# The first RMS norm by halves of the tokens, and the first slabs evicted ahead of the decays

## The chip, the core and the metric

The program runs on one core of a Trainium2 chip. The core has five engines with queues of their own, which meet by semaphores alone: TensorE (PE, with its weight loads as PEld), VectorE (DVE), ScalarE (ACT), GpSimd (POOL) and SyncE (SP). SyncE and ScalarE issue the transfers between HBM and SBUF here. The metric is the device time of one execution in microseconds, the median of several runs.

## The reference

Two transformer blocks over 1024 tokens of width 1024 in float32. The change lies at the start of the first. What is computed there:

```python
h = rms_norm(x, mix_norm_g[l])
p = jnp.einsum("btd,de->bte", h, w_in[l])
(gm_u, gm_v, cv_a, cv_g, dn_q, dn_k, dn_v, dn_g,
 dn_beta, dn_alpha) = jnp.split(p, offsets, axis=-1)
y_a = spatial_gating(gelu(gm_u), gelu(gm_v), ...)
...
beta = jax.nn.sigmoid(beta_logit)
log_alpha = -jnp.exp(a_log) * jax.nn.softplus(alpha_logit + dt_bias)
```

with `rms_norm(x, g) = x * rsqrt(mean(x * x) + 1e-6) * g` over the 1024 features of a token. A convolution branch, a chunked gated delta rule, the output projection and a gated feed-forward follow, then a second block (sliding-window attention beside a state-space layer, between two feed-forwards). None of that is touched.

## The kernel before

**Layout.** Features lie on the 128 partitions and tokens on the free axis: x is 8 tiles k (KD = 8) of 128 features by 1024 tokens, behind 16 columns for meta tokens. The tokens are worked on in two halves of 512, CH1, numbered c = 0, 1.

**Products.** A float32 product is made of three matmuls on operands split in two: high parts by a cast (h_hi, w_hi) and the rests (h_lo, w_lo). Weights come in slabs of 128 output features by 1024 inputs, in pairs (i, j) with j = 0, 1, each j with one buffer for w_raw, w_hi and w_lo. SyncE loads w_raw when GpSimd has split what was there (L486). ScalarE makes w_hi when TensorE is done with the j buffer's slab (w_high, L511 to L517; for pair i it waits for acc_full[j] to count every chunk before). GpSimd makes w_lo in four pieces (L547). TensorE then runs 24 matmuls of 512 columns for each half of the tokens (pe_slab, L651 to L653), having waited for w_lo and for the result bank to be evicted (acc_free).

**The order of the work** is the order in which each engine's instructions are written; no scheduler moves them. The start is:

1. SyncE loads constants, parameters and the first two weight slabs; ScalarE issues the loads of x, two k in each.
2. ScalarE squares tile k over all 1024 tokens into one of two sqx buffers (act_squares, L1060), TensorE sums over the partitions with a matmul against a matrix of 1/1024 (L595), for each half into a PSUM bank.
3. ScalarE casts the first two slabs (L517), takes Sqrt of both halves (L605), and then casts h_hi, eight tiles for each half (L609).
4. VectorE takes, for each half, the reciprocal (L615) and x times gain times reciprocal into one of four tmp buffers (the "gain" below, L625), and makes h_lo of tiles 2 and 5 (L629). GpSimd makes the h_lo of the other six (L583), behind the splits of the first two slabs. A gain that reuses a tmp buffer waits for the h_lo of four tiles before.
5. VectorE casts the 8 columns of weights of beta and alpha into ba_hi and makes ba_lo (L1596, L1597).
6. TensorE, for each half c: the logits of beta and alpha (L1113 to L1115, 24 matmuls), then slabs (0,0) and (0,1) of gm for that half (pe_first_pair, L833). Then eight small transposes of the logits (L1123), slabs (1,0) and (1,1) of gm, slab (0,0) of cv, and the decays' sums, for which it waits.
7. ScalarE copies the logits (L1363, L1365), and runs the chain of decays (Sigmoid, Exp, Ln, Exp, L1368 to L1373, with a table load before each, in turn with VectorE), and only then applies Gelu to the gm slabs (L1380), evicting them, and casts the next pairs.

The other parts of act_mix1, behind the cv slabs, are not touched.

Of the kernel before, what the change touches and what calls it, by code (L numbers as in the profile page):

```python
# [270 lines left out]
def build_program(nc, t):  # L271
    with ExitStack() as ctx:
# [317 lines left out]
        def pe_norm_of_squares(pe, name, chunks):  # L590

            for k in range(KD):
                pe.wait_ge(sem("sqt_" + name), k + 1)
                for c, (c0, w) in enumerate(chunks):
                    ins = pe.matmul(acc[:, c, 0:w], const("mean"), sqx[:, k % 2, c0:c0 + w],  # L595
                                    start=(k == 0), stop=(k == KD - 1), skip_group_check=True)
                    if k == KD - 1:
                        ins.then_inc(sem("ms_" + name), 1)
                if k < KD - 1:
                    ins.then_inc(sem("sqsum_" + name), 1)  # L600

        def act_norm(act, name, chunks):
            for c, (c0, w) in enumerate(chunks):
                act.wait_ge(sem("ms_" + name), c + 1)
                act.activation(rs[:, c0:c0 + w], acc[:, c, 0:w], ACT.Sqrt, bias=const("eps")).then_inc(sem("sd_" + name), 1)  # L605
            for c, (c0, w) in enumerate(chunks):
                for k in range(KD):
                    act.wait_ge(sem("scaled_" + name), c * KD + k + 1)
                    act.copy(h_hi[:, k, c0:c0 + w], tmp[:, k % 4, 0:w]).then_inc(sem("hi_" + name), 1)  # L609
# [444 lines left out]
        def act_squares(act, name, cols, ready):  # L1054

            for k in range(KD):
                ready(k)
                if k >= 2:
                    act.wait_ge(sem("sqsum_" + name), k - 1)
                act.activation(sqx[:, k % 2, cols], x[:, k, cols], ACT.Square).then_inc(sem("sqt_" + name), 1)  # L1060


# [294 lines left out]
        def act_mix1(act):  # L1357
            own = Chain(act, sem("act_own"))
            h_ready(act, 1)
            act.dma_start(gm_par[:, :], t["gm"]).then_inc(sem("gm_par_full"), 16)  # L1360
            for c in range(2):
                aux_wait(act, f"logits_{c}")
                aux_release(act.copy(lgt[0:8, cc(c)], aux(f"logits_{c}")[0:8, :]), f"logits_{c}")  # L1363
            aux_wait(act, "logits")
# [10 lines left out]
            for s in range(4):  # L1375
                i, j = s // 2, s % 2
                for c in range(2):
                    acc_wait(act, SEG["gm"], i, j, c)
# [1210 lines left out]
```

## Time and profile before

| | |
|---|---|
| median of 3 runs | 3810.53 us (3810.5 to 3811.21) |
| the profiled execution | 3814.86 us, span 3813.1 us |
| TensorE busy | 3575.3 us, 94% of the span |
| VectorE, ScalarE, GpSimd busy | 1436.9, 958.9, 1126.2 us |
| mean granted clock of TensorE | 0.975 of full |
| first matmul of a projection | 60.14 us |

Times in the trace count from the start of the span. Granted clock is 1.00 at 2.4 GHz and 0.5 at 1.2 GHz. A row's duration is that of the instructions merged in it (x5 for five); in brackets stands how long the engine had been idle before it and what ended the idle time.

### The profile page before, as it was taken

To read this page: it belongs to the slowest core of one execution; us is meant where nothing else is said; L and a number is where in the kernel's file an instruction comes from. 1 tells how busy PE (TensorE), PEld (TensorE's weight loads), DVE (VectorE), ACT (ScalarE), POOL (GpSimd) and SP (SyncE) were. 2 spreads that over 40 slices of the span, in tenths; PEclk is the share of its full clock that TensorE was granted. 3 is DMA by queue.
4 is the path that set the end of the run, shared out by engine and by line. 5 is a ranking of instruction groups with operands and counts; after the bars stand their busy time and mean duration, and the time that the engine had idled before them with its cause. 6 is when DMAs were issued, how large, how long until landed. Compare 5 with 4: busy or idle time off the path is not lost.

```text
span 3813.1 us, 52558 instructions
## 1 busy us (share of the span) xinstructions
PE 3575.3 (94%) x20104; PEld 2953.9 (77%) x20104; DVE 1436.9 (38%) x2510; ACT 958.9 (25%) x1669; POOL 1126.2 (30%) x1519
## 2 busy tenths in 40 slices
PE   5898889999999989999999989998879999999997
PEld 3677777888888868899999878886657778888885
DVE  3177555221111263421122463736766331121214
ACT  2344343211111142111111332125553321111112
POOL 2233225322222253222222442310004532222223
PEclk8999989999999999999999999999989999999999
DMA  2111212111111121111111321110014211111112
GB/s 85 42 47 32 67 56 82 66 46 50 44 48 47 43 78 60 46 44 44 50 44 46 112 88 63 44 37 32 29 45 161 85 64 44 50 44 52 47 46 92
DMA packets 78700, 219.43 MB, mean 58 GB/s; under 512 B 18896, under 2 KB 19024, under 8 KB 78032
## 3 DMA queue, kind: packets, MB, share of 16 engines
q1 hardware_dynamic: 61536, 173.35, 14.4%
q10 hardware_dynamic: 17008, 43.93, 3.1%
q8 instruction: 107, 1.75, 0.2%
q14 instruction: 49, 0.40, 0.0%
HBM read 196.72 MB, written 19.46 MB: 57 GB/s over the span
## 4 chain that ended last, share of the span: by engine, by line
issue 62%; POOL 23%; PE 9%; DVE 3%; ACT 1%; DMA 1%; POOLq 1%; SPq 0%; ACTq 0%; DVEq 0%
POOL w_lo L547 23%; PE acc L651 2%; PE acc L652 2%; PE acc L653 2%; DVE tmp L625 0%; PE acc L1183 0%; POOLq L552 0%; PE acc L595 0%; DVE cv_acc L1655 0%; PE acc L1178 0%; DVE acc L1733 0%; DVE x_up L1736 0%; PE acc L1297 0%; PE acc L1270 0%; PE acc L1314 0%
## 5 line engine op out<-in xcount | busy, mean ns | idle before, releaser
L547 POOL TENSOR_TENSOR w_lo<-w_raw,w_hi 128x256 fp32r<-128x256 f32 (+3 forms) x1488 | 1086.2, 761 | 2553.7 <-ACT w_hi L517 2553.7
L651 PE MATMUL acc<-h_hi,w_hi 128*128 128x512 f32 (+1 forms) x3552 | 1322.2, 372 | 70.0 <-issue 33.4
L652 PE MATMUL acc<-h_lo,w_hi 128*128 128x512 f32 (+1 forms) x3552 | 1319.3, 371 | 0.0
L653 PE MATMUL acc<-h_hi,w_lo 128*128 128x512 f32 (+1 forms) x3552 | 1313.8, 370 | 0.0
L651 PEld LDWEIGHTS acc<-h_hi,w_hi 128*128 128x128 f32 x3552 | 673.9, 190 | 203.2 <-issue 47.5
L652 PEld LDWEIGHTS acc<-h_lo,w_hi 128*128 128x128 f32 x3552 | 673.4, 190 | 119.7 <-issue 1.9
L653 PEld LDWEIGHTS acc<-h_hi,w_lo 128*128 128x128 f32 x3552 | 673.8, 190 | 117.1
L517 ACT CAST w_hi<-w_raw 128x1024 fp32r<-128x1024 f32 (+3 forms) x372 | 348.3, 937 | 1201.9 <-PE acc L653 1191.7
L920 DVE TENSOR_TENSOR ff_hi<-tmp,acc 128x512 f32 (+3 forms) x154 | 94.5, 613 | 1122.1 <-PE acc L653 1122.1
L651 PE MATMUL acc<-ff_hi,w_hi 128*128 128x512 f32 (+1 forms) x1232 | 450.3, 366 | 21.2 <-POOL w_lo L547 17.0
L653 PE MATMUL acc<-ff_hi,w_lo 128*128 128x512 f32 (+1 forms) x1232 | 447.2, 363 | 0.0
L652 PE MATMUL acc<-ff_lo,w_hi 128*128 128x512 f32 (+1 forms) x1232 | 446.6, 362 | 0.0
L651 PEld LDWEIGHTS acc<-ff_hi,w_hi 128*128 128x128 f32 x1232 | 231.8, 188 | 70.9 <-issue 24.1
L958 DVE SCALAR_TENSOR_TENSOR x<-acc,x 128x512 f32 (+1 forms) x168 | 103.3, 617 | 440.8 <-PE acc L653 439.7
L653 PEld LDWEIGHTS acc<-ff_hi,w_lo 128*128 128x128 f32 x1232 | 231.6, 188 | 38.0
L652 PEld LDWEIGHTS acc<-ff_lo,w_hi 128*128 128x128 f32 x1232 | 231.4, 188 | 38.0 <-issue 0.7
L887 ACT ACTIVATE tmp<-acc 128x512 f32<-128x512 f32 x140 | 75.3, 538 | 551.9 <-PE acc L653 551.8
L792 DVE SCALAR_TENSOR_TENSOR x<-acc,x 128x512 f32<-128x512 f32 (+1 forms) x88 | 56.6, 644 | 205.8 <-PE acc L653 188.5
L925 DVE TENSOR_TENSOR ff_lo<-tmp,ff_hi 128x512 f32 (+3 forms) x154 | 116.4, 756 | 22.2 <-DVE tmp L922 20.0
L922 DVE TENSOR_TENSOR tmp<-tmp,acc 128x512 f32<-128x512 f32 (+1 forms) x154 | 93.4, 606 | 0.0
L1655 DVE SCALAR_TENSOR_TENSOR cv_acc<-cv_y,params,cv_acc 128x1024 f32<-128x1024 f32 x60 | 80.5, 1388 | 0.0
L2199 ACT ACTIVATE sc<-sc,st 128x272 f32<-128x272 f32 (+1 forms) x128 | 64.1, 501 | 24.8 <-DVE st L2428 24.8
(360 smaller groups left out, 2974.5 us busy)
## 6 DMA issues: line engine op xcount, KB each, us to landing
w_raw<-in_ffn_w_dram SPq DMA_DIRECT2D x96, 512.0 KB, 3.4
w_raw<-in_w_in_dram SPq DMA_DIRECT2D x60, 512.0 KB, 3.5
w_raw<-in_w_out_dram SPq DMA_DIRECT2D x32, 512.0 KB, 3.5
w_raw<-in_ffn_w_dram SPq DMA_DIRECT2D x48, 320.0 KB, 2.9
w_raw<-in_w_gate_dram SPq DMA_DIRECT2D x24, 512.0 KB, 3.5
w_raw<-in_w_up_dram SPq DMA_DIRECT2D x24, 512.0 KB, 3.4
w_raw<-in_ffn_w_dram SPq DMA_DIRECT2D x32, 384.0 KB, 3.1
gates_kept<-gstage ACTq DMA_DIRECT2D x32, 256.0 KB, 2.1
```

What stands on the lines that cost most here:

```text
L517: act.copy(w_hi[:, j, 0:width], w_raw[:, j, 0:width]).then_inc(sem("w_high"), 1)
L547: ins = pool.tensor_tensor(w_lo[:, j, a:a + step], w_raw[:, j, a:a + step], w_hi[:, j, a:a + step].bitcast(F32), ALU.subtract)
L651: pe.matmul(bank, wh, rh, start=(k == 0), stop=False)
L652: pe.matmul(bank, wh, rl, start=False, stop=False)
L653: ins = pe.matmul(bank, wl, rh, start=False, stop=(k == seg.kt - 1))
L887: act.activation(tmp[:, c, 0:w], acc[:, c, 0:w], ACT.Silu).then_inc(acc_free[0], 1)
L920: own.mark(dve.tensor_tensor(hi, g, up, ALU.mult))
L922: dve.tensor_tensor(tmp[:, 3:4, 0:w], g, up, ALU.mult).then_inc(acc_free[1], 1)
L925: own.mark(dve.tensor_tensor(ff_lo[:, bass.ds(f, 1), c0:c0 + w], tmp[:, 3:4, 0:w], hi.bitcast(F32), ALU.subtract))
L958: dve.scalar_tensor_tensor(xt, acc[:, 3 * j + c:3 * j + c + 1, 0:w], scale, xt, ALU.mult, ALU.add).then_inc(acc_free[j], 1)
L1655: own.mark(dve.scalar_tensor_tensor(cv_acc[:, ct, :], src, w, cv_acc[:, ct, :], ALU.mult, ALU.add))
L2199: own.mark(act.activation(probs(u, hd), probs(u, hd), ACT.Exp, bias=st[0:nq, b, 0, hd:hd + 1], accum_out=st[0:nq, b, 1, hd:hd + 1]))
```

## The change

- **Load.** The four transfers of x carry four tiles k of one half of the tokens each, first half first (before: two k, all tokens).
- **Norm.** Squares and their sums are made for one half of the tokens at a time: eight squares of 512 columns, Sqrt, the casts of the first two weight slabs; then a square of the second half and a cast of h_hi of the first in turn, eight times; Sqrt of the second half, and its eight casts. TensorE waits for each square and signals each sum. VectorE's and GpSimd's loops over the halves are as before.
- **ba_hi, ba_lo** stand first on VectorE.
- **Evictions.** ScalarE applies Gelu to slabs (0,0) and (0,1) of each half right behind the copy of that half's logits; in the second half the cast of the next slab (1, j) stands ahead of each Gelu. The copy of the transposed logits and the chain of decays follow, then the Gelus of the second pair as before. The wait of ScalarE for the whole norm (h_ready) ahead of gm_par's load goes.

```diff
--- before.py
+++ after.py
@@ -587,26 +587,52 @@
                         split(i, j)
 
 
-        def pe_norm_of_squares(pe, name, chunks):
-
-            for k in range(KD):
-                pe.wait_ge(sem("sqt_" + name), k + 1)
-                for c, (c0, w) in enumerate(chunks):
+        def pe_first_norm(pe):
+
+            for c, (c0, w) in enumerate(CH1):
+                for k in range(KD):
+                    pe.wait_ge(sem("sqt_mix1"), c * KD + k + 1)
                     ins = pe.matmul(acc[:, c, 0:w], const("mean"), sqx[:, k % 2, c0:c0 + w],
                                     start=(k == 0), stop=(k == KD - 1), skip_group_check=True)
-                    if k == KD - 1:
-                        ins.then_inc(sem("ms_" + name), 1)
-                if k < KD - 1:
-                    ins.then_inc(sem("sqsum_" + name), 1)
-
-        def act_norm(act, name, chunks):
-            for c, (c0, w) in enumerate(chunks):
-                act.wait_ge(sem("ms_" + name), c + 1)
-                act.activation(rs[:, c0:c0 + w], acc[:, c, 0:w], ACT.Sqrt, bias=const("eps")).then_inc(sem("sd_" + name), 1)
-            for c, (c0, w) in enumerate(chunks):
-                for k in range(KD):
-                    act.wait_ge(sem("scaled_" + name), c * KD + k + 1)
-                    act.copy(h_hi[:, k, c0:c0 + w], tmp[:, k % 4, 0:w]).then_inc(sem("hi_" + name), 1)
+                    ins.then_inc(sem("sqsum_mix1"), 1)
+
+        def act_first_norm(act):
+
+            for g in range(4):
+                c, k = g // 2, 4 * (g % 2)
+                c0, w = CH1[c]
+                act.dma_start(x[:, k:k + 4, c0:c0 + w], t["x"][:, k:k + 4, c0 - META:c0 - META + w]).then_inc(sem(f"x_full{g}"), 16)
+
+            def square(c, k):
+                c0, w = CH1[c]
+                if k % 4 == 0:
+                    act.wait_ge(sem(f"x_full{2 * c + k // 4}"), 16)
+                if k >= 2:
+                    act.wait_ge(sem("sqsum_mix1"), c * KD + k - 1)
+                act.activation(sqx[:, k % 2, c0:c0 + w], x[:, k, c0:c0 + w], ACT.Square).then_inc(sem("sqt_mix1"), 1)
+
+            def root(c):
+                c0, w = CH1[c]
+                act.wait_ge(sem("sqsum_mix1"), (c + 1) * KD)
+                act.activation(rs[:, c0:c0 + w], acc[:, c, 0:w], ACT.Sqrt, bias=const("eps")).then_inc(sem("sd_mix1"), 1)
+
+            def high(c, k):
+                c0, w = CH1[c]
+                act.wait_ge(sem("scaled_mix1"), c * KD + k + 1)
+                act.copy(h_hi[:, k, c0:c0 + w], tmp[:, k % 4, 0:w]).then_inc(sem("hi_mix1"), 1)
+
+            act.wait_ge(sem("params_full"), 32)
+            for k in range(KD):
+                square(0, k)
+            root(0)
+            for j in range(2):
+                w_high(act, SEG["gm"], 0, j)
+            for k in range(KD):
+                square(1, k)
+                high(0, k)
+            root(1)
+            for k in range(KD):
+                high(1, k)
 
         def dve_norm(dve, own, name, chunks, gain):
 
@@ -1050,15 +1076,6 @@
                         own.mark(dve.scalar_tensor_tensor(x[:, k, cols], x[:, k, cols], param("final_g")[:, k:k + 1], rs[:, cols],
                                                           ALU.mult, ALU.mult))
                 own.wait()
-
-        def act_squares(act, name, cols, ready):
-
-            for k in range(KD):
-                ready(k)
-                if k >= 2:
-                    act.wait_ge(sem("sqsum_" + name), k - 1)
-                act.activation(sqx[:, k % 2, cols], x[:, k, cols], ACT.Square).then_inc(sem("sqt_" + name), 1)
-
 
         def flat(a, b):
             return small[:, a:b, :].rearrange("p a b -> p (a b)")
@@ -1356,11 +1373,19 @@
 
         def act_mix1(act):
             own = Chain(act, sem("act_own"))
-            h_ready(act, 1)
             act.dma_start(gm_par[:, :], t["gm"]).then_inc(sem("gm_par_full"), 16)
+
+            def first_pair(j, c):
+                acc_wait(act, SEG["gm"], 0, j, c)
+                act.activation(gm_u[:, j, cc(c)], acc[:, 3 * j + c, :], ACT.Gelu).then_inc(acc_free[j], 1)
+
             for c in range(2):
                 aux_wait(act, f"logits_{c}")
                 aux_release(act.copy(lgt[0:8, cc(c)], aux(f"logits_{c}")[0:8, :]), f"logits_{c}")
+                for j in range(2):
+                    if c:
+                        w_after(act, SEG["gm"], 0, j)
+                    first_pair(j, c)
             aux_wait(act, "logits")
             aux_release(act.copy(logits, aux("logits")[:, 0:64]), "logits")
             act.wait_ge(aux_free[EVENT["logits"][0]], EVENT["logits"][1] + 1)
@@ -1372,13 +1397,11 @@
             own.link(act.activation(z_ln, z_ln, ACT.Ln, bias=ones[:, 0:1]))
             own.link(act.activation(rate[:, 0:4], param("a_log"), ACT.Exp))
             act.sem_inc(sem("z_ln_full"), 1)
-            for s in range(4):
-                i, j = s // 2, s % 2
+            for j in range(2):
                 for c in range(2):
-                    acc_wait(act, SEG["gm"], i, j, c)
-                    dst = (gm_u if i == 0 else gm_v)[:, j, cc(c)]
-                    act.activation(dst, acc[:, 3 * j + c, :], ACT.Gelu).then_inc(acc_free[j], 1)
-                w_after(act, SEG["gm"], i, j)
+                    acc_wait(act, SEG["gm"], 1, j, c)
+                    act.activation(gm_v[:, j, cc(c)], acc[:, 3 * j + c, :], ACT.Gelu).then_inc(acc_free[j], 1)
+                w_after(act, SEG["gm"], 1, j)
             for j in range(2):
                 act.wait_ge(acc_free[j], chunk_no(SEG["gm"], 1, 1) + 1)
             act.sem_inc(sem("gm_full"), 8)
@@ -1593,10 +1616,6 @@
             return second_half
 
         def dve_mix1(dve, own):
-            own.link(dve.tensor_copy(ba_hi[:, :, :], param("w_ba").rearrange("p (k e) -> p k e", k=KD)))
-            own.link(dve.tensor_tensor(ba_lo[:, :, :], param("w_ba").rearrange("p (k e) -> p k e", k=KD),
-                                       ba_hi[:, :, :].bitcast(F32), ALU.subtract))
-            dve.sem_inc(sem("ba_full"), 1)
             dve.wait_ge(sem("logits_full"), 1)
             z3 = z_a.rearrange(by_head, h=4)
             own.link(dve.tensor_tensor(z3, logits.rearrange("p (n e) -> p n e", e=8)[:, :, 4:8],
@@ -2490,20 +2509,10 @@
         @block.scalar
         def _(act):
 
-            for k in range(0, KD, 2):
-                act.dma_start(x[:, k:k + 2, REAL], t["x"][:, k:k + 2, :]).then_inc(sem(f"x_full{k // 2}"), 16)
-
-            def loaded(k):
-                act.wait_ge(sem(f"x_full{k // 2}"), 16)
-
             def keep():
                 act.dma_start(t["x_kept"], x[:, :, :]).then_inc(sem("x_stored"), 16)
 
-            act.wait_ge(sem("params_full"), 32)
-            act_squares(act, "mix1", REAL, loaded)
-            for j in range(2):
-                w_high(act, SEG["gm"], 0, j)
-            act_norm(act, "mix1", CH1)
+            act_first_norm(act)
             second_half = act_mix1(act)
             act_turn(act, "ffn0", (SEG["out1a"], SEG["out1b"]), beside=second_half)
             act_ffn(act, "ffn0", CH1, lambda i: act_meta(act, i))
@@ -2521,6 +2530,10 @@
 
             own = Chain(dve, sem("dve_own"))
             dve.wait_ge(sem("params_full"), 32)
+            own.link(dve.tensor_copy(ba_hi[:, :, :], param("w_ba").rearrange("p (k e) -> p k e", k=KD)))
+            own.link(dve.tensor_tensor(ba_lo[:, :, :], param("w_ba").rearrange("p (k e) -> p k e", k=KD),
+                                       ba_hi[:, :, :].bitcast(F32), ALU.subtract))
+            dve.sem_inc(sem("ba_full"), 1)
             dve_norm(dve, own, "mix1", CH1, param("mix_g"))
             dve_mix1(dve, own)
             dve_ffn(dve, own, "ffn0", CH1, 1.0, lambda i: dve_meta(dve, own, i))
@@ -2535,7 +2548,7 @@
         def _(pe):
 
             pe.wait_ge(sem("params_full"), 32)
-            pe_norm_of_squares(pe, "mix1", CH1)
+            pe_first_norm(pe)
             pe_mix1(pe)
             pe_ffn(pe, "ffn0", CH1, "ffn1", lambda: pe_meta(pe))
             pe_ffn(pe, "ffn1", CH2, "mix2", lambda: pe_fin(pe))
```

ScalarE's norm before, as its instructions stand (`sqx` squares, `rs` Sqrt, `h_hi` casts of the normed tokens, `w_hi` casts of the weight slabs; a semaphore waited for in brackets):

```order
L1060 ACT_TABLE_LOAD [waits x_full0]
L1060 ACTIVATE sqx<-x 128x1024 [waits params_full]
L1060 ACTIVATE sqx<-x 128x1024 [waits x_full0]
L1060 ACTIVATE sqx<-x 128x1024 [waits sqsum_mix1,x_full1] x2
L1060 ACTIVATE sqx<-x 128x1024 [waits sqsum_mix1,x_full2] x2
L1060 ACTIVATE sqx<-x 128x1024 [waits sqsum_mix1,x_full3] x2
L517 CAST w_hi<-w_raw 128x1024 [waits raw_full0]
L517 CAST w_hi<-w_raw 128x1024 [waits raw_full1]
L605 ACT_TABLE_LOAD
L605 ACTIVATE rs<-acc,consts 128x512 [waits ms_mix1] x2
L609 CAST h_hi<-tmp 128x512 [waits scaled_mix1] x16
```

and the same place now, up to the second of eight turns of square and cast:

```order
L612 ACTIVATE sqx<-x 128x512
L612 ACTIVATE sqx<-x 128x512 [waits sqsum_mix1] x2
L612 ACTIVATE sqx<-x 128x512 [waits sqsum_mix1,x_full1]
L612 ACTIVATE sqx<-x 128x512 [waits sqsum_mix1] x3
L617 ACT_TABLE_LOAD
L617 ACTIVATE rs<-acc,consts 128x512 [waits sqsum_mix1]
L517 CAST w_hi<-w_raw 128x1024 [waits raw_full0]
L517 CAST w_hi<-w_raw 128x1024 [waits raw_full1]
L612 ACTIVATE sqx<-x 128x512 [waits x_full2]
L622 CAST h_hi<-tmp 128x512 [waits scaled_mix1]
L612 ACTIVATE sqx<-x 128x512
L622 CAST h_hi<-tmp 128x512 [waits scaled_mix1]
```

The Sqrt of the first half and the table load for it moved ahead of the weight casts, and the second half's squares between the casts of h_hi. The Sqrt of the second half has no table load.

ScalarE's evictions of the first gm pair before (`lgt` and `small<-acc` the logits, `gm_u` the Gelus of pair 0):

```order
L1363 COPY lgt<-acc 8x512 [waits aux_full1]
L1365 COPY small<-acc 128x64 [waits aux_full0]
L1368 ACT_TABLE_LOAD [waits aux_free0]
L1368 ACTIVATE small<-small 128x32
L1371 ACT_TABLE_LOAD
L1371 ACTIVATE small<-small 128x32 [waits z_full]
L1372 ACT_TABLE_LOAD
L1372 ACTIVATE small<-small,consts 128x32 [waits act_own]
L1373 ACT_TABLE_LOAD
L1373 ACTIVATE small<-params 128x4 [waits act_own]
L1380 ACT_TABLE_LOAD [waits act_own]
L1380 ACTIVATE gm_u<-acc 128x512 [waits acc_full0] x2
```

and now:

```order
L1384 COPY lgt<-acc 8x512 [waits aux_full0]
L1380 ACT_TABLE_LOAD
L1380 ACTIVATE gm_u<-acc 128x512 [waits acc_full0]
L1380 ACTIVATE gm_u<-acc 128x512 [waits acc_full1]
L1384 COPY lgt<-acc 8x512 [waits aux_full1]
L517 CAST w_hi<-w_raw 128x1024 [waits acc_full0,raw_full0]
L1380 ACTIVATE gm_u<-acc 128x512 [waits acc_full0]
L517 CAST w_hi<-w_raw 128x1024 [waits acc_full1,raw_full1]
L1380 ACTIVATE gm_u<-acc 128x512 [waits acc_full1]
L1390 COPY small<-acc 128x64 [waits aux_full0]
L1393 ACT_TABLE_LOAD [waits aux_free0]
L1393 ACTIVATE small<-small 128x32
```

The casts of the next pair and the Gelus of the first moved ahead of the chain of decays.

## Rows read from the trace of the kernel before

**Rows 1.** Timeline of TensorE, 60 to 84 us (start, duration, instruction, idle before).
```profile
60.14 0.59 PE L1113 MATMUL acc<-h_hi,ba_hi 128*8 128x512 f32 x1 [32.67 <-DVEq L1599]
...
78.56 0.40 PE L1113 MATMUL acc<-h_hi,ba_hi 128*8 128x512 f32 x1
```

**Rows 2.** Timeline of all engines, 95 to 110 us.
```profile
95.32 0.66 PE L1123 MATMUL acc<-consts,lgt 8*128 8x8 f32 x8
...
103.95 1.09 ACT L1380 ACTIVATE gm_u<-acc 128x512 f32<-128x512 f32 x2
104.92 1.05 ACT L517 CAST w_hi<-w_raw 128x1024 fp32r<-128x1024 f32 x1
...
106.04 4.14 POOL L547 TENSOR_TENSOR w_lo<-w_raw,w_hi 128x256 fp32r<-128x256 f32 x6 [46.19 <-ACT w_hi L517]
...
108.86 0.80 PE L651 MATMUL acc<-h_hi,w_hi 128*128 128x512 f32 x1 [12.88 <-POOL w_lo L547]
```

**Rows 3.** Windows: length, busy time of each engine (instructions), granted clock, DMA share, GB/s.
```profile
28.00:60.00 32.00, 0.00 (x0) 0.00 (x0) 30.36 (x24) 11.52 (x19) 22.98 (x18) 0.53 0.10 33
...
68.00:96.00 28.00, 27.98 (x127) 20.07 (x125) 0.00 (x0) 0.80 (x2) 0.00 (x0) 1.00 0.00 1
...
110.00:400.00 290.00, 277.26 (x1345) 226.09 (x1344) 175.37 (x200) 111.33 (x175) 89.82 (x79) 0.96 0.15 46
```

**Rows 4.** Timeline of ScalarE, 0 to 30 us.
```profile
8.32 1.28 ACT L1060 ACT_TABLE_LOAD   x1 [8.32 <-DMA x<-in_x_dram]
9.62 2.00 ACT L1060 ACTIVATE sqx<-x 128x1024 f32<-128x1024 f32 x2
14.66 1.06 ACT L1060 ACTIVATE sqx<-x 128x1024 f32<-128x1024 f32 x1 [3.05 <-PE acc L595]
...
28.38 1.26 ACT L605 ACTIVATE rs<-acc,consts 128x512 f32<-128x512 f32 x2
```

**Rows 5.** Timeline of VectorE, 25 to 60 us.
```profile
29.18 3.35 DVE L615 RECIPROCAL rs<-rs 128x512 f32<-128x512 f32 x1 [29.18 <-ACT rs L605]
32.56 5.42 DVE L625 SCALAR_TENSOR_TENSOR tmp<-x,params,rs 128x512 f32<-128x512 f32 x5
37.91 1.75 DVE L629 TENSOR_TENSOR h_lo<-tmp,h_hi 128x512 fp32r<-128x512 f32 x1
...
43.41 3.35 DVE L615 RECIPROCAL rs<-rs 128x512 f32<-128x512 f32 x1
...
58.72 1.22 DVE L1597 TENSOR_TENSOR ba_lo<-params,ba_hi 128x64 fp32r<-128x64 f32 x1
```

**Rows 6.** Timeline of GpSimd, 25 to 60 us.
```profile
26.20 5.49 POOL L547 TENSOR_TENSOR w_lo<-w_raw,w_hi 128x256 fp32r<-128x256 f32 x8 [25.74 <-ACT w_hi L517]
34.04 6.74 POOL L583 TENSOR_TENSOR h_lo<-tmp,h_hi 128x512 fp32r<-128x512 f32 x4 [2.35 <-ACT h_hi L609]
42.72 2.91 POOL L583 TENSOR_TENSOR h_lo<-tmp,h_hi 128x512 fp32r<-128x512 f32 x2 [1.94 <-ACT h_hi L609]
...
56.95 2.90 POOL L583 TENSOR_TENSOR h_lo<-tmp,h_hi 128x512 fp32r<-128x512 f32 x2 [1.94 <-ACT h_hi L609]
```

**Rows 7.** The page's DMA issues: count, size of each, microseconds to landing.
```profile
gates_kept<-gstage ACTq DMA_DIRECT2D x32, 256.0 KB, 2.1
```

**Rows 8.** Timeline of weight loads (PEld) of the sums of squares.
```profile
15.22 0.33 PEld L595 LDWEIGHTS acc<-sqx,consts 128*128 128x128 f32 x1 [0.52 <-issue]
16.07 0.26 PEld L595 LDWEIGHTS acc<-sqx,consts 128*128 128x128 f32 x1 [0.52 <-issue]
16.57 0.19 PEld L595 LDWEIGHTS acc<-sqx,consts 128*128 128x128 f32 x1 [0.24 <-issue]
17.00 0.19 PEld L595 LDWEIGHTS acc<-sqx,consts 128*128 128x128 f32 x1 [0.24 <-issue]
```

**Rows 9.** Groups by form, GpSimd, 400 to 3800 us: count, busy, mean ns.
```profile
L547 POOL TENSOR_TENSOR w_lo<-w_raw,w_hi 128x256 fp32r<-128x256 f32 x852 | 677.2, 826 | 1569.8 <-ACT w_hi L517 1569.8
```

**Rows 10.** Timeline of ScalarE, behind 108 us.
```profile
116.05 0.60 ACT L1380 ACTIVATE gm_v<-acc 128x512 f32<-128x512 f32 x1 [8.17 <-PE acc L653]
```

## The prediction, made before the changed kernel was run

> **What bounds the kernel now.** I read the timeline of TensorE first, since the page has it busy most of the span: it shows where it stands still and what released it. Two rows matter. The first projection matmul starts at 60.14 us after 32.67 us of waiting, released by VectorE's queue at L1599, the signal that ba_hi and ba_lo are there [rows 1]. The first slab of the second gm pair starts at 108.86 us after 12.88 us of waiting for w_lo [rows 2]. From 110 to 400 us TensorE is busy 277.26 of 290 us [rows 3]: behind this start it is the bound, so time taken off the two waits should come off the end. Then I read the timelines of ScalarE, VectorE and GpSimd for what stands before each wait, and the windows for the granted clock.
>
> The first wait: squares on ScalarE from 9.62, Sqrt at 28.38 [rows 4], reciprocal at 29.18, gains from 32.56 [rows 5], h_lo on GpSimd from 34.04, the first half's last piece ending at 42.72 + 2.91 = 45.63 [rows 6]. The first half is usable at 45.63, but VectorE makes ba_lo only behind the second half, ending 58.72 + 1.22 = 59.94, so TensorE starts both halves' work then. The second wait: the cast of the next weights waits on ScalarE behind the chain of decays, from the transposes' end at 95.32 + 0.66 = 95.98 to the first Gelu at 103.95, then 104.92 (cast), 106.04 (split), 108.86 [rows 2].
>
> **The change part by part.**
>
> *ba_hi and ba_lo first on VectorE.* They need only the parameters; ba_lo takes 1.22 us, ba_hi about as much, and VectorE is idle until 29.18 [rows 5]. Price nothing; TensorE's first half is then bound by its own norm alone.
>
> *Input by halves.* Four transfers of 1024 KB as before, rows of 2048 B for 4096 B. Bytes ahead of x_full0 are the same, so ScalarE starts at 8.32 again [rows 4]. Shorter rows are unseen for this load; the nearest row is the 256 KB store of gstage, 2048 B for each partition, landing in 2.1 us [rows 7]. I take 0; the bounds are -0.5 and +2.0 us (that row's whole landing again).
>
> *First half's norm.* A square of 1024 columns takes 1.06 us; I take 0.6 for 512 (the 512-column Sqrt pair takes 1.26). The matmuls of one k for both halves took 3.4 us at first: weight loads 0.85 us apart, two for each f32 matmul, four for each k, then 0.43 apart from about 16 us [rows 8]. A half costs 1.7 and later 0.86 us for each k. Started at about 10.3: k0 to k2 end by 15.8, the rise falls into k3 (16.6), and four more at 0.86 end at 20.0. The table load for Sqrt has no wait of its own now and stands right behind the last square: 18.9 to 20.15. Sqrt then starts at 20.15 for 28.38 before, the reciprocal 0.8 later at 20.95, the first gain 3.38 later at 24.3 (32.56 before). On GpSimd nothing is saved by as much: its eight weight pieces (5.49 us [rows 6]) follow the casts, which now stand behind Sqrt: 21.9 to about 27.6, beside the gains. Where VectorE and GpSimd both subtract or multiply SBUF tiles, pieces take 6.74 / 4 = 1.68 us, and the last two 2.91, so some 1.23 for the one that runs alone [rows 6]; and weight pieces average 0.826 us later in the kernel against 5.49 / 8 = 0.69 here [rows 6, 9]. So I let the four gains beside the splits take 1.68 us each and not 0.67: the fifth starts at 31.0 for 36.2 before (1.68 before the h_lo at 37.91 [rows 5]). From there the pattern is that of before (32.56 to 45.63 is 13.07, of which 3.7 lies before the fifth gain): 31.0 + 9.4 = 40.4, and 0.4 more, since the casts of h_hi now take turns with squares: first half ready at 40.8. Without any such slowing it would be 38.5, the lower bound.
>
> *Second half's squares between the casts.* Each square needs the matmul of two k before. TensorE has stood still from 20.0 to 23.5 and starts low (28 to 60 us before, behind the same sums, has 0.53 of full clock [rows 3]). At 1.7 us a matmul the chain keeps pace with VectorE's 1.68 us steps. Following it k by k, the last square ends at 38.3, its matmul at about 39.5; Sqrt without a load, reciprocal at 40.5. The second half then repeats 43.41 to 56.95 + 2.90 = 59.85, which is 16.44 us [rows 5, 6]: ready at 57.0.
>
> The Trainium skill, page "ScalarE: Activation LUTs", section "What ACT_TABLE_LOAD costs", adds a drain of about 1.38 us to the 1.28 us of a load. Here an activation follows its load 1.30 us after the load's start (8.32 and 9.62) [rows 4]; by the page the Sqrt of the first half would be an estimated 1.4 us later and the gain that much smaller. I go by the row.
>
> *TensorE.* Before, half one's logits and slabs took 78.56 - 60.14 = 18.42 us and half two's 95.32 - 78.56 = 16.76 for the same count [rows 1, 2], so a start at the low clock costs 1.66. After, TensorE has just done the squares' sums and stands still for 1.5 us only; I take it to be still high: 40.8 + 16.7 = 57.5, just above the 57.0 at which half two is ready. Half two's work, then transposes: 57.5 + 16.76 + 0.66 = 74.9.
>
> *First slabs evicted ahead of the decays.* ScalarE casts the next weights as soon as slab (0,0) is done in both halves, at 57.5 + 11.1 = 68.6; by the distances 104.92, 106.04, 108.86 [rows 2] w_lo is there 3.94 later, at 72.6, so TensorE goes straight on at 74.9. The slack is 2.3 us. The chain of decays (7.97 us) now lies beside slabs (1,0), (1,1) and (cv 0,0), 33 us of matmuls; TensorE wants the decays only behind them. Evictions of (1,0) queue behind the chain until about 83 and are wanted at 97. gm_par's load is issued behind the last cast, near 56, and wanted behind the decays. Should that cover go, the price is at most the 8 us of the chain.
>
> *Sum.* 108.86 - 74.9 = 34.0. Before, that slab's first chunk took 116.05 - 108.86 = 7.19 us [rows 2, 10]; 24 matmuls at the high clock take 5.56 (16.7 / 72 each), and now it follows on work without a pause: 1.6 more. Together 35.6 us. The profiled execution took 3814.86 us (span 3813.1): 3779.3 by it. The median of the runs is 3810.53, 4.3 lower; my forecast for it is 3775.
>
> **The rivals.**
>
> *Larger, 38 us or more (3772):* VectorE and GpSimd don't slow each other at the splits. First half at 38.5, then 55.2, 72.6: gain 37.9. For it: the reciprocal beside the splits took the same 3.35 us; against it: 1.68 us pieces.
>
> *The turns on ScalarE slow both halves (3781):* a cast of h_hi stands behind a square, which stands behind a matmul at 1.2 GHz. If TensorE never leaves the low clock there, each k costs 1.7 + 0.6 = 2.3 us instead of 1.68: eight times 0.62 is 5.0 us on half one, and half two and TensorE's first chunk follow, the latter at 18.42. Gain 35.6 - 5.0 - about 1 = 29 to 30. For it: TensorE has little to do for each k. Against it: two squares are in flight. The Trainium skill, page "TensorE: Matmul & The Clock Gate", section "HAM oscillation — how this bites in real kernels", describes such short work between waits that never gets the high clock; here the squares' sums rose to it after some 5 us although ScalarE was in the loop [rows 8], so by the row they rise again, by the page they may not.
>
> *The second wait stays in part (3788):* if ScalarE reaches the cast over 2.3 us late, TensorE stops before slab (1,0); at 10 us late with a low clock after it, gain 35.6 - 10 - 1.7 = 24.
>
> *Given back later (3809):* some wait behind 110 us isn't moved by an earlier start. Against it: every transfer and engine there is released by TensorE's own progress.
>
> *Slower (above 3818):* the longer dense run of TensorE gets less clock. Each 512-column matmul of the projections then takes twice its 0.23 us; after 155 of them the gain is gone, after 188 there is a loss of 7.6 us. Against it: 68 to 96 us is dense at 1.00 [rows 3].
>
> **How the numbers follow.** Forecast 69%, larger 8%, slow turns 15%, second wait 5%, given back 1.5%, slower 1.5%. The likeliest's own range is 3773 to 3777: it takes in the low clock in chunk one (1.7 us less gain) and small errors of mine. The 8 in 10 range reaches over the larger case and the slow turns with the bound of 2 us for the load: 3770 to 3783. A difference of 0.2% (7.6 us) is about what a measurement of this kernel can tell from none; the first four cases are faster by more: 0.97, within 0.2% 0.015, slower 0.015.
>
> **What the changed profile would show.** Right: ba_lo before 12 us; Sqrt of half one near 20; first projection matmul near 41, released by h_lo or VectorE's signal; no wait of TensorE between the chunks; slab (1,0) at 75, with no wait for w_lo; everything after 110 us shifted evenly. Wrong: a first matmul after 44 (slow turns), a wait for w_lo near 75, a second half later than 59, or a stage after 110 us longer than before.

## The result and the profile after

| | before | changed |
|---|---|---|
| median of 5 runs | 3811.2 us | 3786.5 us (3783.6 to 3792.8) |
| ratio | | 0.9933, 95% interval 0.9917 to 0.9949 |
| profiled execution, span | 3814.9, 3813.1 us | 3792.0, 3789.8 us |
| first projection matmul | 60.14 us | 42.06 us |
| gm slab (1,0) | 108.86 us | 76.08 us |
| cv slab (0,1) | 148.95 us | 115.69 us |
| from there to the end | 3664.2 us | 3674.1 us |

The change gains 25 us (19 to 32 by the interval); 35.6 were forecast, with a range of 28 to 41. At cv slab (0,1) the changed profile is 33.3 us ahead, at the end 23.3. So the question is where 10 us went behind the place that was changed. The time from cv slab (0,1) to the end is called the rest below; "clock" is TensorE's granted clock.

The start first. ScalarE's timeline of the changed kernel (start, duration; the view of [rows 4]):

```profile
10.57 1.28 ACT L612 ACT_TABLE_LOAD   x1 [10.57 <-DMA x<-in_x_dram]
11.87 1.15 ACT L612 ACTIVATE sqx<-x 128x512 f32<-128x512 f32 x2
...
20.99 1.28 ACT L617 ACT_TABLE_LOAD   x1
22.28 0.69 ACT L617 ACTIVATE rs<-acc,consts 128x512 f32<-128x512 f32 x1
```

The load releases ScalarE 2.25 us later than before; from there to Sqrt the steps took what was worked out (11.71 us, 11.83 forecast), and Sqrt follows its table load by 1.29 us. The Trainium skill's drain behind a load ("ScalarE: Activation LUTs", "What ACT_TABLE_LOAD costs") doesn't show: the Sqrt would have started later by it.

VectorE (ba_lo, reciprocal, four gains, the fifth, the second reciprocal; the view of [rows 5]):

```profile
8.23 0.23 DVE L2534 TENSOR_TENSOR ba_lo<-params,ba_hi 128x64 fp32r<-128x64 f32 x1
23.00 3.35 DVE L641 RECIPROCAL rs<-rs 128x512 f32<-128x512 f32 x1 [14.55 <-ACT rs L617]
26.39 4.33 DVE L651 SCALAR_TENSOR_TENSOR tmp<-x,params,rs 128x512 f32<-128x512 f32 x4
32.58 1.74 DVE L651 SCALAR_TENSOR_TENSOR tmp<-x,params,rs 128x512 f32<-128x512 f32 x1 [1.86 <-POOL h_lo L583]
...
41.83 3.35 DVE L641 RECIPROCAL rs<-rs 128x512 f32<-128x512 f32 x1 [2.24 <-ACT rs L617]
```

and GpSimd (weight pieces, then h_lo of both halves, then slab (1,0)'s pieces; the view of [rows 6]):

```profile
23.98 7.33 POOL L547 TENSOR_TENSOR w_lo<-w_raw,w_hi 128x256 fp32r<-128x256 f32 x8 [23.52 <-ACT w_hi L517]
31.27 5.85 POOL L583 TENSOR_TENSOR h_lo<-tmp,h_hi 128x512 fp32r<-128x512 f32 x4
39.44 2.52 POOL L583 TENSOR_TENSOR h_lo<-tmp,h_hi 128x512 fp32r<-128x512 f32 x2 [2.32 <-ACT h_hi L622]
...
55.50 2.94 POOL L583 TENSOR_TENSOR h_lo<-tmp,h_hi 128x512 fp32r<-128x512 f32 x2 [1.95 <-ACT h_hi L622]
71.22 2.82 POOL L547 TENSOR_TENSOR w_lo<-w_raw,w_hi 128x256 fp32r<-128x256 f32 x4 [12.78 <-ACT w_hi L517]
```

The four gains beside the weight pieces took 1.08 us each in the mean, less than the 1.68 I gave them. The pieces paid instead, 7.33 us for the eight where they took 5.49 before. Only four of the eight did: the first four stood beside the reciprocal, and four alone take 2.78 us (a row of the kernel with the late split, below); that leaves 4.55 us for the other four, 1.14 each. The fifth gain waited for the first h_lo behind them. The first half is ready at 39.44 + 2.52 = 41.96, the second at 55.50 + 2.94 = 58.44 (forecast 40.8 and 57.0: both late by no more than the load was). w_lo of slab (1,0) is there at 71.22 + 2.82 = 74.04.

TensorE, the last sums of squares and the first projection matmul:

```profile
38.90 2.17 PE L595 MATMUL acc<-sqx,consts 128*128 128x512 f32 x4 [2.22 <-ACT sqx L612]
42.06 0.40 PE L1130 MATMUL acc<-h_hi,ba_hi 128*8 128x512 f32 x1 [0.99 <-issue]
```

and around slab (1,0), TensorE and ScalarE (the view of [rows 2]):

```profile
75.49 0.66 PE L1140 MATMUL acc<-consts,lgt 8*128 8x8 f32 x8
75.65 1.05 ACT L517 CAST w_hi<-w_raw 128x1024 fp32r<-128x1024 f32 x1 [4.01 <-PE acc L679]
...
76.08 0.51 PE L677 MATMUL acc<-h_hi,w_hi 128*128 128x512 f32 x1
```

These four matmuls took 2.17 us at a clock of 1.00; with it low for most of them they took 3.41 (second profile, below). Slab (1,0) starts without a wait, 0.6 us behind the start of the transposes. Up to here 32.8 of the 34.0 us are there.

### The profile page after: what moved, and what is told of

It reads as the page before. It is cut to its first block, busy times and chain, and to the rows that moved or that the text cites. A ratio compares the mean times of both kernels' runs of the same rounds, so it can differ in the third digit from the quotient of the medians.

```text
span 3789.8 us, 52561 instructions
## 1 busy us (share of the span) xinstructions
PE 3584.7 (95%) x20104; PEld 2960.5 (78%) x20104; DVE 1437.8 (38%) x2510; ACT 963.5 (25%) x1678; POOL 1128.6 (30%) x1519
## 4 chain that ended last, share of the span: by engine, by line
issue 62%; POOL 24%; PE 9%; DVE 2%; ACT 1%; DMA 1%; POOLq 1%; SPq 0%; ACTq 0%; DVEq 0%
POOL w_lo L547 23%; PE acc L677 2%; PE acc L678 2%; PE acc L679 2%; PE acc L1200 0%; POOLq L552 0%; DVE cv_acc L1674 0%; DVE acc L1752 0%; PE acc L1195 0%; DVE x_up L1755 0%; PE acc L1314 0%; PE acc L595 0%; DMA x<-in_x_dram 0%; PE acc L1287 0%; PE acc L1257 0%
```

## Where 10 us went

The same stretch of work, from cv slab (0,1) to the end, in a window of each profile (length, then busy time of TensorE, its weight loads, VectorE, ScalarE, GpSimd; clock, DMA share, GB/s; the view of [rows 3]). Before:

```profile
148.95:3813.10 3664.15, 3485.30 (x19757) 2893.35 (x19755) 1403.81 (x2476) 912.62 (x1605) 1087.28 (x1475) 0.98 0.18 57
```

Changed, and a shorter window of it that is used below:

```profile
115.69:3789.80 3674.11, 3493.10 (x19756) 2900.31 (x19754) 1404.14 (x2474) 914.79 (x1605) 1088.86 (x1475) 0.98 0.18 57
2130.00:2160.00 30.00, 23.68 (x109) 19.21 (x108) 19.13 (x25) 10.83 (x17) 18.34 (x23) 0.89 0.40 148
```

TensorE runs the same 19,757 instructions (one record less in the second trace), and is busy for 3493.1 us instead of 3485.3; it stands still for 181.0 instead of 178.8. So there is no new wait of note: 7.8 of the 10 us are matmuls that ran slower. Worked out from the traces' records of the granted clock, the matmul time behind this point that fell into low stretches (1.2 GHz) is 112.5 us for 95.7 before; half of the difference is 8.4, so the clock accounts for all of the 7.8.

The shorter window shows one place. From 2130 to 2160 us the changed kernel had 0.89 of the clock and 109 matmul records; before, a window as long that starts at about the same work:

```profile
2158.30:2188.30 30.00, 24.67 (x130) 19.68 (x129) 20.44 (x27) 12.15 (x19) 18.45 (x24) 1.00 0.47 178
```

had 1.00 and 130, the further work included that the other window no longer reaches. Both have pauses of about 2 us for w_lo there; in the changed trace the matmuls behind this one start 0.43 us apart and more, where 0.23 is the step at the high clock:

```profile
2143.35 0.79 PE L677 MATMUL acc<-ff_hi,w_hi 128*128 128x512 f32 x1 [2.16 <-POOL w_lo L547]
2143.94 0.63 PE L678 MATMUL acc<-ff_lo,w_hi 128*128 128x512 f32 x1
```

The first such place is the pause for the gm transposes just ahead of cv slab (0,1). It lasts 2.34 us in both traces. Before:

```profile
147.21 1.13 PE L1140 MATMUL acc<-consts,gm_v 128*128 128x128 f32 x8 [2.34 <-ACT small L1393]
148.54 0.66 PE L1140 MATMUL acc<-consts,gm_v 128*128 128x128 f32 x4 [0.20 <-ACT gm_t L1396]
148.95 0.48 PE L651 MATMUL acc<-h_hi,w_hi 128*128 128x512 f32 x1
149.27 0.39 PE L652 MATMUL acc<-h_lo,w_hi 128*128 128x512 f32 x1
```

and changed:

```profile
113.13 2.91 PE L1157 MATMUL acc<-consts,gm_v 128*128 128x128 f32 x12 [2.34 <-ACT small L1416]
115.69 0.78 PE L677 MATMUL acc<-h_hi,w_hi 128*128 128x512 f32 x1
116.26 0.63 PE L678 MATMUL acc<-h_lo,w_hi 128*128 128x512 f32 x1
```

The matmuls behind it start 0.22 to 0.32 us apart before, and 0.43 and more now, with the clock at 0.69 in the mean from 111 to 122 us and at 1.00 from 144 to 155 before. Equal pause, equal work, other clock. The lead over the kernel before tells it in steps: 34.1 us at the second chunk of slab (1,0) (81.77 for 115.85) and still at the transposes behind the pause (113.13 for 147.21), 33.3 at cv slab (0,1), 23.3 at the end.

Two readings are open from here; the expectations call them theory 1 and theory 2. They count the rest from slightly other places (3663 to 3663.8 and 3672.4 to 3673.9 us for the first two profiles); in the text it is always counted from the start of cv slab (0,1), 3664.2 and 3674.1. Either the clock's low stretches fall by chance, and the rest scatters from run to run; or the earlier start itself brings a longer rest, the same each time.

## Experiments

**Parts of the change.** Only ba_hi and ba_lo first, moved here from dve_mix1:

```diff
             dve.wait_ge(sem("params_full"), 32)
+            own.link(dve.tensor_copy(ba_hi ...))
+            own.link(dve.tensor_tensor(ba_lo ...))
+            dve.sem_inc(sem("ba_full"), 1)
             dve_norm(dve, own, "mix1", CH1, param("mix_g"))
```

> The kernel before with ba_hi and ba_lo first on VectorE, nothing else. Local effect, both theories: the first projection matmul starts near 45.7 instead of 60.1 (14.4 earlier), slab (1,0) of gm near 94.5 instead of 108.9, its wait of 12.9 us for w_lo stays. Theory 1 (clock by chance): what lies behind the cv slab (0,1), 3663 us in the trace of before and 3672 in that of the changed kernel, differs from run to run by up to 10 us with the time that TensorE's clock is low, whatever the start; the median gain is 14 us within 5. Theory 2 (an earlier start lengthens what follows, systematically): the rest is longer than 3663 us in proportion to the shift, the median gain is 9 to 10 us.

Ratio 0.9959 (0.9945 to 0.9972), 15.6 us. The first projection matmul came at 44.65, 1.0 us earlier than expected, and the second wait stays:

```profile
93.28 0.79 PE L651 MATMUL acc<-h_hi,w_hi 128*128 128x512 f32 x1 [12.88 <-POOL w_lo L547]
```

Only the evictions moved (act_mix1 as in the changed kernel behind its wait for the whole norm; the norm as before):

```diff
             for c in range(2):
                 aux_wait(act, f"logits_{c}")
                 aux_release(act.copy(lgt ...))
+                for j in range(2):
+                    if c:
+                        w_after(act, SEG["gm"], 0, j)
+                    first_pair(j, c)
...
```

> The kernel before with only the evictions moved: the first gm slabs are evicted and the next weights cast ahead of the chain of decays. First projection matmul at 60.1 as before; slab (1,0) of gm at 96.0 instead of 108.9 without a wait for w_lo. Its first chunk takes 5.6 instead of 7.2 us, since no low clock follows a wait. Local gain 14.5 us. Theory 1: median gain 14.5 within 5, the rest behind cv slab (0,1) anywhere from 3660 to 3673 us. Theory 2: the rest is longer than 3663 by 3 to 5 us, median gain about 10.

Ratio 0.9964 (0.9951 to 0.9978), 13.7 us. No wait is left at slab (1,0):

```profile
94.42 0.51 PE L651 MATMUL acc<-h_hi,w_hi 128*128 128x512 f32 x1
```

The changed kernel with the evictions as before, and ScalarE's wait for the whole norm ahead of them as before:

```diff
-                for j in range(2):
-                    if c:
-                        w_after(act, SEG["gm"], 0, j)
-                    first_pair(j, c)
...
```

> The changed kernel with ScalarE's evictions as before: load and norm by halves and ba first, but the first gm slabs evicted behind the decays. First projection matmul near 42, slab (1,0) of gm near 89 after a wait of about 12.9 us. Local gain 19.7 us. Theory 1: median gain 20 within 5. Theory 2: 14 to 15 us.

Ratio 0.9964 (0.995 to 0.9978), 13.7 us; slab (1,0) at 89.10, cv slab (0,1) at 129.25. Locally each part gave what it should: 13.6, 15.7 and 19.7 us at cv slab (0,1), and 33.3 for all. The end times don't follow: the third is 6.1 us ahead of the first there and ends level with it. The three rests (3658.0, 3664.1, 3663.6 us) are not longer in proportion to the shift: against the reading that an earlier start by itself lengthens the rest. The gains don't decide by themselves: the first two fit theory 1 and the first contradicts theory 2 (9 to 10 us), but the third, 13.7 us by the ratio and 15.2 by the medians, is what theory 2 said (14 to 15) and at or below the edge of theory 1 (20 within 5).

**The two kernels again.** The changed one:

> The changed kernel once more, unaltered, for a second profile and a second set of runs. The start should be equal to the first profile's within 1 us (first projection matmul at 42.1, slab (1,0) near 76.1). Theory 1: the rest behind cv slab (0,1), 3672.4 us in the first profile, comes out different by some us, following the time at the low clock (174 us in the first profile, 194 in that of before, much of it idle). Theory 2: it is 3672 again within 1 us.

Ratio 0.9928 (0.9914 to 0.9941), rest 3670.6 us. The start agrees less well than expected: slab (1,0) came at 77.75, 1.7 later. The clock was low again at the last sums of squares (0.50 from 39 to 42 us), so the second half came late and TensorE waited for it:

```profile
39.50 3.41 PE L595 MATMUL acc<-sqx,consts 128*128 128x512 f32 x4 [2.22 <-ACT sqx L612]
...
60.40 0.39 PE L1130 MATMUL acc<-h_hi,ba_hi 128*8 128x512 f32 x1 [0.85 <-POOL h_lo L583]
```

And the one before:

> The kernel before once more, unaltered, for a second profile. Theory 1 (which short pauses of TensorE are followed by a low clock varies from run to run): what lies behind cv slab (0,1), 3663.8 us in the first profile, comes out different by some us, with the time of matmuls at the low clock, and that span less half of this time is 3616 to 3619 us again, as in the six profiles so far. Theory 2 (the changed kernel's later part is longer by its own making): 3664 again within 1 us, where the two of the changed kernel had 3673.9 and 3670.3.

Rest 3667.6 us for 3664.2 the first time: the rest isn't fixed by the kernel, and the reading that it is falls in its strict form. The kernel before took 3805.2 to 3819.6 us in 55 timed runs. In the 50 of them beside the experiments, whose clock is on record (3805.2 to 3818.6 us), the mean granted clock was 0.978 in the fastest and 0.973 to 0.974 in the slowest.

**Time shifted by idle work.** Four, eight and twelve matmuls more ahead of slab (1,0), here the four:

```diff
+            pe.wait_ge(split_done, 3)
+            pe.wait_ge(acc_free[0], SEG["gm"].need[1, 0, 0])
+            for _ in range(4):
+                pe.matmul(acc[:, SEG["gm"].bank(1, 0, 0), 0:512], w_hi[:, 0, 0:P], h_hi[:, 0, META:META + 512], start=True, stop=False,
+                          skip_group_check=True)
             for j in range(2):
                 pe_slab(pe, SEG["gm"], 1, j, h)
```

> The changed kernel with 4 idle matmuls of 512 columns (each repeats the first matmul of gm slab (1,0), which then starts afresh) ahead of slab (1,0): 4 x 0.23 = 0.9 us of added work, in dense work of TensorE, so that all behind it comes 0.9 us later against the moments at which the clock falls and rises. Theory 1 (how these moments meet the short pauses decides how much low clock follows, and the changed kernel meets it badly): the rest behind cv slab (0,1) changes by several us either way; the median need not rise by 0.9 us, and of the three kernels padded by 4, 8 and 12 at least one is faster than the changed kernel (3786). Theory 3 (the changed kernel's rest is 7 us longer than that of before for another reason, such as its code): the median rises by what is added, to 3787.

> The same with 8 idle matmuls, 1.9 us of added work. Theory 1: a change of the rest by several us, either way. Theory 3: median 3788.

> The same with 12 idle matmuls, 2.8 us of added work. Theory 1: a change of the rest by several us, either way. Theory 3: median 3789.

Ratios 0.9928, 0.9934 and 0.9929, medians 3783.3, 3783.7 and 3781.9, on a chip where the kernel before took 3810.2: level with the changed kernel, and no sign of the 0.9 to 2.8 us of added work, though intervals of 0.13% (5 us) would not exclude it. The profiles say more. Rest after 12 added matmuls:

```profile
118.48:3778.90 3660.42, 3481.60 (x19757) 2890.55 (x19755) 1404.46 (x2476) 912.59 (x1605) 1087.89 (x1475) 0.98 0.17 57
```

3660.4 us with 3481.6 busy, 13.7 us less than the changed kernel's first profile. All fourteen profiles, from cv slab (0,1) to the end. "Low" is the matmul time in low stretches of the clock, worked out from the traces' clock records; the last column is an estimate, the mean span of the timed runs less the place of cv slab (0,1) in the profile (which moved by 1.7 us between the two profiles of the changed kernel):

| kernel | rest us | TensorE busy | still | low | rest, timed runs |
|---|---|---|---|---|---|
| before, twice | 3664.2, 3667.6 | 3485.3, 3488.0 | 178.8, 179.6 | 95.7, 101.4 | 3661.8 (50 runs) |
| ba first / evictions only / halves | 3658.0 / 3664.1 / 3663.6 | 3478.3 / 3484.4 / 3485.1 | 179.7 / 179.7 / 178.5 | 81.7 / 94.2 / 94.3 | 3659.4 / 3664.3 / 3667.0 |
| changed, twice | 3674.1, 3670.6 | 3493.1, 3491.1 | 181.0, 179.5 | 112.5, 108.2 | 3668.3 (10 runs) |
| changed + 4 / 8 / 12 matmuls | 3667.4 / 3662.3 / 3660.4 | 3488.9 / 3483.2 / 3481.6 | 178.5 / 179.2 / 178.8 | 104.5 / 90.3 / 87.5 | 3665.9 / 3665.7 / 3662.9 |
| loads in pairs / split late | 3663.9 / 3660.7 | 3485.0 / 3481.4 | 178.9 / 179.2 | 94.6 / 88.5 | 3662.1 / 3663.2 |
| both of these, twice | 3653.6, 3663.9 | 3472.7, 3485.4 | 180.8, 178.6 | 68.1, 95.7 | 3661.9 (8 runs) |

The waits are equal within 2.5 us. The rest moves by 20 us, with the busy time of equal work, and within one kernel by 10 (last row). Busy time less half of the low time is 3436.7 to 3438.7 us in all fourteen: equal work takes equal time but for the clock, which leaves nothing for a cause such as the kernel's code (theory 3 of the padded kernels).

But the rest isn't the same for every kernel on average either. By the last column the changed kernel's is 6.5 us longer than that of the kernel before, with a standard error of 1.3 (0.5 for before, 1.2 for the changed one, 0.9 to 2.8 for the others), while that of both edits together, which start earlier still, is not longer at all. So a part of the 10 us is this kernel's own, the rest of it the draw of one profile.

The pause of 2.34 us ahead of cv slab (0,1) stands in every profile. In the 12 us from 4 before that slab, the clock was 0.72 in the mean in three of them (the changed kernel twice, both edits the first time), 0.86 in two (ba first, 8 matmuls) and 1.00 in nine. The kernel with both edits shows it both ways, first and second profile:

```profile
107.98 2.90 PE L1159 MATMUL acc<-consts,gm_v 128*128 128x128 f32 x12 [2.34 <-ACT small L1418]
```

```profile
107.63 1.13 PE L1159 MATMUL acc<-consts,gm_v 128*128 128x128 f32 x8 [2.34 <-ACT small L1418]
```

**The load.** First half in four transfers:

```diff
-            for g in range(4):
-                c, k = g // 2, 4 * (g % 2)
+            for g in range(6):
+                c, k, n = ((0, 0, 2), (0, 2, 2), (0, 4, 2), (0, 6, 2), (1, 0, 4), (1, 4, 4))[g]
```

> The changed kernel with its first half loaded as four transfers of 512 KB (two tiles k each) in place of two of 1024 KB; the second half as before, two of 1024 KB. In the changed kernel the first 1024 KB of x, now in rows of 2048 B, landed at 10.5 us instead of 8.3, though the whole load ended at about the same time: if its queue gets as many packets and not as many bytes as SyncE's (rows of 4096 B and more), the first tiles come late. Theory 1: with 512 KB in front, ScalarE starts at about 8.0, when the parameters are there, and all up to the first projection matmul is some 2 us earlier (40 instead of 42.1). Theory 2 (the issue of the transfers, 4.8 us for the last one, holds ScalarE up): no change, since as many or more are to be issued. End time: 2 us or less, within the scatter of the low clock.

The first transfer's time from issue to landing (1024 KB), before:

```profile
DMA to landing us min/median/max: 7.5/7.5/7.5
```

changed, in rows of 2048 B:

```profile
DMA to landing us min/median/max: 9.7/9.7/9.7
```

and ScalarE of this experiment:

```profile
0.76 5.66 ACTq L604 DMA_DIRECT2D x<-in_x_dram  x6
6.73 1.28 ACT L612 ACT_TABLE_LOAD   x1 [6.73 <-DMA x<-in_x_dram]
8.02 1.15 ACT L612 ACTIVATE sqx<-x 128x512 f32<-128x512 f32 x2
```

The first 512 KB land at 6.7, ScalarE's table load starts 3.8 us earlier and its first square 3.9, and the first projection matmul comes at 38.97, slab (1,0) at 74.59. Six issues took 5.66 us of queue time and held nothing up, so the cause is the landing. Ratio 0.9905 (0.9888 to 0.9922). That the other queue's longer rows take a larger share is the explanation that fits, not one that was isolated.

**The second slab's split behind the first half's h_lo:**

```diff
-                for j in range(2):
+                for j in range(1 if name == "gm" else 2):
                     split(0, j)
...
+                    if name == "gm" and c == 0:
+                        split(0, 1)
```

> The changed kernel with GpSimd's split of the second weight slab moved behind the first half's six h_lo tiles (it is wanted 5.5 us after those). In the changed kernel the eight weight pieces took 7.33 us and ended at 31.27 with the first cast h_hi waiting since 28.0. Expected: first projection matmul near 39 instead of 42.1, no wait for w_lo at the second slab, second half ready near 57 instead of 58.4; since TensorE then waits for the second half, slab (1,0) is 1 to 2 us earlier, not 3. Theory 2 (VectorE's chain, not GpSimd's, sets the first half): first matmul within 0.5 us of 42.1.

GpSimd in it:

```profile
24.78 2.78 POOL L547 TENSOR_TENSOR w_lo<-w_raw,w_hi 128x256 fp32r<-128x256 f32 x4 [24.31 <-ACT w_hi L517]
28.83 3.41 POOL L583 TENSOR_TENSOR h_lo<-tmp,h_hi 128x512 fp32r<-128x512 f32 x2 [1.28 <-ACT h_hi L624]
32.67 2.94 POOL L583 TENSOR_TENSOR h_lo<-tmp,h_hi 128x512 fp32r<-128x512 f32 x2 [0.42 <-ACT h_hi L624]
37.93 2.52 POOL L583 TENSOR_TENSOR h_lo<-tmp,h_hi 128x512 fp32r<-128x512 f32 x2 [2.32 <-ACT h_hi L624]
40.40 2.83 POOL L547 TENSOR_TENSOR w_lo<-w_raw,w_hi 128x256 fp32r<-128x256 f32 x4
```

Half one was ready at 40.45 and the first matmul came at 40.56: 1.5 us earlier, half of the 3 expected, since now h_lo waits for ScalarE's casts (1.28 and 0.42 us) in their turns with squares. Slab (1,0) at 74.56. Ratio 0.9911 (0.9897 to 0.9924).

**Both edits.**

> Both edits of the two kernels above together: loads of two tiles in front, and the split of the second slab late. Expected: first projection matmul near 37, second half ready near 55, slab (1,0) of gm near 72.5 instead of 76.1. End time 3 us below the changed kernel's if the low clock falls alike; its scatter (3783.6 to 3792.8 in ten runs of the changed kernel) may hide it.

> The kernel with both edits (loads of two tiles in front, the split of the second slab late) once more, unaltered: its four timed runs lay between 3766.3 and 3778.7 us. Start as in its first profile (first projection matmul near 37, slab (1,0) near 71) within the 1.5 us that the first low clock moves. Theory 1: the rest behind cv slab (0,1), 3653.1 us in the first profile, comes out longer this time, between 3655 and 3665, and the median lies between 3770 and 3780. Theory 3 (a kernel's rest is its own): 3653 again, and a median near 3766.

First matmul and slab (1,0) in the first of them:

```profile
36.93 0.40 PE L1132 MATMUL acc<-h_hi,ba_hi 128*8 128x512 f32 x1 [0.99 <-issue]
```

```profile
70.93 0.51 PE L679 MATMUL acc<-h_hi,w_hi 128*128 128x512 f32 x1
```

That is 5.1 us ahead of the changed kernel, where 3.6 were expected. Ratios 0.9903 (0.9888 to 0.9918) and 0.9890 (0.9872 to 0.9908), medians 3775.3 and 3774.0: the fastest kernel here, 37 to 42 us below the one before. The rests of its two profiles, 3653.6 and 3663.9, once more differ within one kernel, and the second median lay where theory 1 had it: the faster profile had luck, not a better rest.

## Why the prediction was wrong

- *The two waits, and what they were worth:* right. Both are gone, each part gives its share alone, and the start is 1.2 us later than forecast at slab (1,0).
- *Input by halves at price 0:* wrong by 2.25 us, just beyond my bound of 2.0. The row I took for it, a store of 256 KB elsewhere in the kernel, says nothing of a load beside another queue's; that the two queues' sharing is the cause was not isolated.
- *Gains at 1.68 us beside the splits:* too dear (1.08 in the mean), and the splits too cheap (5.7 for 7.33). The two errors met within 1 us, so that of the load's 2.25 us only 1.16 were left at the first half's end. That is luck.
- *Slow turns:* this didn't set the time, but it wasn't absent. In the first profile the clock was low from 27 to 34 us and high from then on to slab (1,0), as the rows said; in the second it fell once more, from 39 to 42 us, and slab (1,0) came 1.7 us later. The Trainium skill ("TensorE: Matmul & The Clock Gate", "HAM oscillation — how this bites in real kernels") tells of a clock that falls again in each wait between short bursts of matmuls, with waits of 3 to 5 us; the second profile agrees in part, with two low stretches and waits of 1.0 to 3.3 us.
- *The slab's first chunk, 1.6 us for a high clock:* 1.3 in its place (second chunk at 81.77 for 115.85, less the lead of 32.8), and 0.8 of it taken back at the next pause, where the changed trace fell to the low clock and the one before hadn't.
- *The second wait stays in part:* its heading says 3788, its sum (a gain of 24) 3786.5, which is what was measured. That is chance: TensorE didn't wait ahead of slab (1,0).
- *The step that failed:* "everything after 110 us shifted evenly", the ground on which "given back later" got 1.5%. I excluded a wait that doesn't move, rightly. But work between equal waits isn't of equal length: it depends on where the clock falls. The sum had no term for it. In the profiles the rest came out 10.0 us longer, and in the timed runs 6.5 on average; the forecast took one profile of before and three close runs (3810.5 to 3811.2) for its whole scatter. Of the forecast lead of 35.6 us, 34.1 was there at the second chunk of slab (1,0), 33.3 at cv slab (0,1) and 23.3 at the end.

Shown: the 10 us are slower matmuls and not waits; the rest of one kernel varies by as much; and the changed kernel's rest is longer on average (3668.3 us in ten runs for 3661.8 in fifty), which by the profiles means more work at the low clock. Open: what in the start picks this. It isn't the size of the shift, as both edits together start 5 us earlier and have a rest of 3661.9, and the kernels padded by 0.9 to 2.8 us lie between.

## What to carry to other kernels

In a kernel like this one, bound by TensorE with many short pauses, a gain at the start arrives at the end only within what the clock does to the work behind it. Put into the range of the forecast what one kernel differs by between runs (14 us here in 55), and some us more for a new start. Before looking for a new wait, compare busy times of equal work, each less half of its matmul time at the low clock: what is left should agree (within 2 us here). When a transfer is cut into shorter rows beside another queue's load, its first piece may come later (9.7 us for 7.5 here); a small piece in front took this back.

## What the hardware showed unexpectedly

- After equal pauses of 2.34 us the clock stayed high in nine profiles and was low in five, in one kernel both ways.
- ba_hi and ba_lo took 1.05 and 1.22 us at 57.6 us, beside GpSimd's h_lo, and 0.20 and 0.23 us at 8.0 us with GpSimd idle.
- Beside each other, a 128x512 gain and a 128x256 weight piece take about 1.14 us each, for 0.67 and 0.69 alone, while gain and 128x512 h_lo take 1.68 each. The reciprocal slowed nothing: 3.35 us with the pieces beside it, and they kept their 0.69.
